# Half of the z projection inside the normalising loop, and a new order of small steps in the attention passes

## The reference, cut to what matters

```
h = rmsnorm(x, norm_pre)                       # 2048 rows of 1024
proj = h @ w_in                                # z | x,B,C | dt | q | k | v | z_sb | gates
xbc = silu(causal_conv4(xbc)); dt = softplus(dt_raw + dt_bias)
y = ssd_scan(...)                              # chunks, state carried from chunk to chunk
y = gated_group_rmsnorm(y, z, ...)             # y * silu(z), z is 2048 x 1024
o = stick_breaking(q, k, v)                    # softplus pass, sums, exponential pass, times v
out = x + rmsnorm((g1 * (y @ Wssd) + g2 * (o*silu(z_sb) @ Wsb)) @ Wout)
```

## Time and profile before

| | us |
|---|---|
| median of 3 runs | 1501.82 (1501.56 to 1502.63) |
| the profiled execution, its own time | 1497.82 |
| span of its slowest core (core 2) | 1495.9 |
| spans of the 8 cores | 1484.8 to 1495.9 |

### The profile page before, as it was taken

One profiled execution on the slowest core, in us unless ns is written; L12 is line 12 of the kernel. 1 busy time (PEld: TensorE's weight loads), 2 busy tenths in 40 slices (PEclk: granted clock), 3 DMA queues, 4 the chain that ended last, 5 costly groups with the idle time before them and its releaser, 6 DMA issues.

```text
span 1495.9 us, 22674 instructions; the slowest of 8 cores (1484.8 to 1495.9 us)
## 1 busy us (share of the span) xinstructions
PE 1286.3 (86%) x7112; PEld 539.3 (36%) x7236; DVE 833.3 (56%) x1386; ACT 858.8 (57%) x1081; POOL 106.6 (7%) x187
## 2 busy tenths in 40 slices
PE   2778987889889879889879889888777989999997
PEld 1434444323234323233323333323223434444443
DVE  2566852756756766766766666676563222322356
ACT  5446652776776776686776676777674321212122
POOL 2200000001000001000000000001001000000022
PEclk9989998999999999999999999998879999999999
DMA  9732664312121313121211012015103952153263
GB/s 238 121 72 53 106 141 103 63 35 52 53 49 42 63 34 67 39 48 56 50 34 62 29 35 62 29 35 103 44 15 72 215 108 29 15 71 29 71 225 155
DMA packets 117635, 109.34 MB, mean 73 GB/s; under 512 B 67984, under 2 KB 96016, under 8 KB 117520
## 3 DMA queue, kind: packets, MB, share of 16 engines
q1 hardware_dynamic: 65376, 83.51, 18.1%
q0 software_dynamic: 52144, 24.38, 14.2%
HBM read 103.81 MB, written 28.44 MB: 88 GB/s over the span
## 4 chain that ended last, share of the span: by engine, by line
PE 62%; ACT 18%; issue 8%; DVE 6%; DMA 5%; SPq 0%; ACTq 0%; DVEq 0%; POOL 0%; POOLq 0%
PE ps L311 15%; PE ps L1013 9%; ACT wtb L1063 9%; PE ps L1023 7%; PE ps L1029 5%; PE ps L396 5%; ACT spF L1063 4%; PE ps L1241 4%; PE ps L1210 4%; PE ps L317 4%; PE ps L1215 4%; PE ps L1080 3%; PE ps L377 3%; ACT spD L1063 2%; DMA wst<-w_in 2%
## 5 line engine op out<-in xcount | busy, mean ns | idle before, releaser
L1063 ACT ACTIVATE wtb<-ps 128x1024 bf16<-128x1024 f32 (+2 forms) x320 | 272.0, 893 | 186.4 <-PE ps L1029 172.9
L1013 PE MATMUL ps<-qT,kT 64*128 64x512 bf16 (+3 forms) x1280 | 235.5, 369 | 105.2 <-ACT wtb L1063 35.1
L311 PE MATMUL ps<-hT,wst 128*128 128x512 bf16 x1128 | 262.2, 385 | 17.8 <-DMA wst<-w_in 4.9
L1063 ACT ACTIVATE spF<-ps 128x1024 bf16<-128x1024 f32 x192 | 184.4, 1036 | 19.4 <-PE ps L1013 19.2
L1013 PEld LDWEIGHTS ps<-qT,kT 64*128 64x128 bf16 x1280 | 69.4, 93 | 280.9 <-issue 275.9
L311 PEld LDWEIGHTS ps<-hT,wst 128*128 128x128 bf16 x1152 | 113.0, 99 | 155.9 <-issue 26.9
L396 PE MATMUL ps<-hT,wst 128*128 128x512 bf16 x467 | 149.4, 396 | 12.5 <-DVE yB L842 8.7
L1029 PE MATMUL ps<-Ssum,cb 128*128 128x512 bf16 (+2 forms) x512 | 143.0, 361 | 0.0
L1224 ACT ACTIVATE gs<-ps,bgate 128x512 f32<-128x512 f32 x64 | 44.0, 688 | 172.4 <-PE ps L311 139.6
L1227 DVE TENSOR_TENSOR tt<-ps,gs 128x512 f32<-128x512 f32 x64 | 44.2, 691 | 160.2 <-ACT gs L1224 160.2
L1048 DVE TENSOR_TENSOR Ssum<-Ssum,spF 128x1024 bf16<-128x1024 bf16 x168 | 115.6, 688 | 15.1 <-DVE Ssum L1048 6.7
(11 more groups left out here) (124 smaller groups left out, 1521.6 us busy)
## 6 DMA issues: line engine op xcount, KB each, us to landing
seg<-cs_rows SPq DMA_DIRECT2D x32, 512.0 KB, 4.3
wst<-w_in POOLq DMA_DIRECT2D x32, 256.0 KB, 5.5
wst<-w_in POOLq DMA_DIRECT2D x5, 1024.0 KB, 13.2
region<-x SPq DMA_DIRECT2D x8, 512.0 KB, 13.3
xmore<-x SPq DMA_DIRECT2D x8, 512.0 KB, 13.8
sz_rows<-zst SPq DMA_DIRECT2D x16, 256.0 KB, 2.3
xs_rows<-xst SPq DMA_DIRECT2D x16, 256.0 KB, 3.2
xsc<-xs_rows SPq DMA_DIRECT2D x16, 256.0 KB, 2.9
```

What stands on the lines that cost most here:

```text
L311: K.op("pe", lambda e, c=c: e.matmul(ps[bank][:], lhsT=wt[:, c, coff:coff + 128], rhs=hT[:, c, g * 512:(g + 1) * 512], start=(c == 0), sto ...
L1013: K.op("pe", lambda e, a_=a_, pr=pr: e.matmul(ps[b0 + a_][:, q0:512], lhsT=kT[par][pr, c * 128:(c + 1) * 128], rhs=qT[par][pr, qs:qs + nq] ...
L1063: K.op("act", lambda e: e.activation(out=dst, in_=psall[:, b0:b0 + 2, q0:512], func=fn), r=[B_ps[b0], B_ps[b0 + 1]], w=[bd])
```

## The change

Four edits. (1) The z units take a row tile and a half. The 15 units of half 0 of tiles 0 to 14 are issued in the normalising loop, two in each of iterations 8 to 14 and one in 15; the other 17 stay in the convolution stage, spread more thinly. `zst` becomes four buffers of one unit each, each stored by its own DMA, and the weights of half 0 are loaded at t = 3. (2) `dt_proj` uses bank 1. (3) In phase 1 the scan step and the fill are issued ahead of `post`. (4) `sub` and `lim` of the next chunk are appended to elements 8, 9 and 10 of `ex_`, the load of its rows moves from element 7 to 2, and `sp_` is one element shorter; chunk 0 keeps them in `sp_` behind four empty elements.

```diff
-    def z_unit(u):
-        t, hf = u // 2, u % 2
-        bank = 6 + hf
+    def z_unit(t, hf):
+        k_ = zn[0] % 4
+        bank = 6 + zn[0] % 2
+        zn[0] += 1
         proj_tok(wz, [B_wz[hf]], hf * 512, 512, t, ps[bank][:], bank)
...
-            if hf == 1: K.dma("sp", sz_dr[t * 128:(t + 1) * 128, :], zs[:], r=bz, w=[B_szd[t]])
+        K.op("act", lambda e: e.activation(out=zst[k_][:], in_=ps[bank][:], func=AF.Silu), r=[B_ps[bank]], w=[B_zst[k_]])
+        K.dma("sp", sz_dr[t * 128:(t + 1) * 128, hf * 512:(hf + 1) * 512], zst[k_][:], r=[B_zst[k_]], w=[B_szd[t][hf]])
@@ dt_proj
-            proj_tok(wz, [B_wz[2]], 1024, 16, t, ps[6][:, t * 16:(t + 1) * 16], 6)
+            proj_tok(wz, [B_wz[2]], 1024, 16, t, ps[1][:, t * 16:(t + 1) * 16], 1)
@@ normalising loop
         if t >= 0:
             a_evac(t)
+        if t == 3:
+            K.dma("pool", wz[:, :, 0:512], w_in_v[:, :, 0:512], r=[B_hT[1]], w=[B_wz[0]])
         if t == 11:
...
-            for hf in range(2):
-                K.dma("pool", wz[:, :, hf * 512:(hf + 1) * 512], w_in_v[:, :, hf * 512:(hf + 1) * 512], w=[B_wz[hf]])
+            K.dma("pool", wz[:, :, 512:1024], w_in_v[:, :, 512:1024], w=[B_wz[1]])
         if t >= 4 and t % 4 < 3:
             proj_g(t % 4, t // 4 - 1, "dve")
+        if t >= 8:
+            z_unit(2 * (t - 8), 0)
+            if t < NT - 1:
+                z_unit(2 * (t - 8) + 1, 0)
@@ convolution stage
-    zq = list(range(32))
+    zq = [(15, 0)] + [(t, 1) for t in range(NT)]
         if 3 <= nb < 12:
-            z_units(1)
             proj_g(nb, 2, "act")
             proj_g(nb, 3, "act")
             z_units(1)
         if i == 0:
             dt_proj()
-            z_units(2)
+            z_units(1)
...
-            z_units(6)
+            z_units(4)
@@ scan lists
-        sp_ = [[(sub, 0)], [(sub, 1), (scores,)], [(mscf,)], [(lim, 0), (lim, 1)], [(yoff, 0), (xwf,)], [(yoffm, 0)],
-               [(yoff, 1), (yinit, 0)], [(yoffm, 1)], [(state, 0)], [(statea, 0)], [(state, 1), (yinit, 1)], [(statea, 1)],
-               [(yadd, 0)], [(yadd, 1)], [(nextload,)]]
-        ex_ = [[(expo, 0)], [(expo, 1), (attn, 0)], [(attn, 1)], [(diag, 0)], [(diaga, 0)], [(diag, 1)], [(diaga, 1), (gate, 0)],
-               [(gate, 1), (sq, 0), (nextseg,)], [(sq, 1)], [(norm, 0), (norm, 1)], [], [(tr,)], [(ev,)]]
+        pre_ = [[(sub, 0)], [(sub, 1)], [(lim, 0), (lim, 1)]]
+        sp_ = [[(scores,)], [(mscf,)], [(yoff, 0)], [(yoffm, 0)], [(yoff, 1), (xwf,)], [(yoffm, 1)], [(yinit, 0)],
+               [(state, 0)], [(statea, 0)], [(state, 1), (yinit, 1)], [(statea, 1)], [(yadd, 0)], [(yadd, 1)], [(nextload,)]]
+        ex_ = [[(expo, 0)], [(expo, 1), (attn, 0)], [(attn, 1), (nextseg,)], [(diag, 0)], [(diaga, 0)], [(diag, 1)],
+               [(diaga, 1), (gate, 0)], [(gate, 1), (sq, 0)], [(sq, 1)], [(norm, 0), (norm, 1)], [], [(tr,)], [(ev,)]]
+        if c == 0:
+            sp_ = [[], [], [], []] + pre_ + sp_
@@ attention loop
+                if lists:
+                    for m_, k_ in zip(lists[0][0], (8, 9, 10)):
+                        ex_[k_] = ex_[k_] + m_
                 queue += ex_
...
-        for T in (groups[gi - 2] if gi >= 2 else []):
-            post(T)
         if ph == 1:
             used = run_micro(queue.pop(0)) if queue else False
             ...
+        for T in (groups[gi - 2] if gi >= 2 else []):
+            post(T)
+        if ph == 1:
             for T in grp:
                 prep_qk(T)
```

More of the change, by code:

```diff
@@ L455, in build @@
     sz_dr = nc.dram_tensor("sz_rows", [L, 1024], BF16).ap()
-    B_szd = [Buf() for _ in range(NT)]
+    B_szd = [[Buf(), Buf()] for _ in range(NT)]
     xs_dr = nc.dram_tensor("xs_rows", [L, 1024], BF16).ap()
@@ L485, in build @@
     B_xcT = [Buf(), Buf()]
-    zst = [sb("zst%d" % i, [128, 1024], BF16) for i in range(2)]
-    B_zst = [[Buf(), Buf()] for _ in range(2)]
+    zst = [sb("zst%d" % i, [128, 512], BF16) for i in range(4)]
+    B_zst = [Buf() for _ in range(4)]
+    zn = [0]
     xst = [sb("xst%d" % i, [128, 8, 128], BF16) for i in range(4)]
@@ L591, in dt_proj @@
         for t in range(NT):
-            proj_tok(wz, [B_wz[2]], 1024, 16, t, ps[6][:, t * 16:(t + 1) * 16], 6)
-        K.op("dve", lambda e: e.tensor_tensor(out=dts[:, 0, :, :], in0=ps[6][:, 0:NT * 16].rearrange("p (t h) -> p t h", t=NT),
+            proj_tok(wz, [B_wz[2]], 1024, 16, t, ps[1][:, t * 16:(t + 1) * 16], 1)
+        K.op("dve", lambda e: e.tensor_tensor(out=dts[:, 0, :, :], in0=ps[1][:, 0:NT * 16].rearrange("p (t h) -> p t h", t=NT),
                                               in1=hv[:, 0:16].unsqueeze(1).to_broadcast([128, NT, 16]), op=ALU.add),
-             r=[B_ps[6], B_hv], w=[B_dts] + B_xbuf)
+             r=[B_ps[1], B_hv], w=[B_dts] + B_xbuf)
         K.op("dve", lambda e: e.tensor_scalar(out=dts[:, 2, :, :], in0=dts[:, 0, :, :], scalar1=-1.0, scalar2=None, op0=ALU.mult),
@@ L690, in z_units @@
             if zq:
-                z_unit(zq.pop(0))
+                z_unit(*zq.pop(0))
     ident(0)
@@ L793, in load_chunk @@
         K.dma("sp", btk[k_][:], bt_dr[rows, :], r=[B_btd[b][half] for b in range(2)], w=[B_btk[k_]])
-        K.dma("sp", sz[k_][:], sz_dr[rows, :], r=[B_szd[c]], w=[B_sz[k_]])
+        K.dma("sp", sz[k_][:], sz_dr[rows, :], r=B_szd[c], w=[B_sz[k_]])
     def heads(ap):
@@ L950, in nextseg @@
                 load_seg(c + 1)
-        sp_ = [[(sub, 0)], [(sub, 1), (scores,)], [(mscf,)], [(lim, 0), (lim, 1)], [(yoff, 0), (xwf,)], [(yoffm, 0)],
-               [(yoff, 1), (yinit, 0)], [(yoffm, 1)], [(state, 0)], [(statea, 0)], [(state, 1), (yinit, 1)], [(statea, 1)],
-               [(yadd, 0)], [(yadd, 1)], [(nextload,)]]
-        ex_ = [[(expo, 0)], [(expo, 1), (attn, 0)], [(attn, 1)], [(diag, 0)], [(diaga, 0)], [(diag, 1)], [(diaga, 1), (gate, 0)],
-               [(gate, 1), (sq, 0), (nextseg,)], [(sq, 1)], [(norm, 0), (norm, 1)], [], [(tr,)], [(ev,)]]
-        return sp_, ex_
+        pre_ = [[(sub, 0)], [(sub, 1)], [(lim, 0), (lim, 1)]]
[5 more added lines that the diff above has]
+            sp_ = [[], [], [], []] + pre_ + sp_
+        return pre_, sp_, ex_
     def run_micro(m):
@@ L1089, in build @@
     queue = []
-    chunk = [0]
+    lists = [ssd_lists(c) for c in range(NT)]
     for gi in range(len(groups) + 2):
@@ L1098, in build @@
             if ph == 0:
-                sp_, ex_ = ssd_lists(chunk[0])
-                chunk[0] += 1
+                pre_, sp_, ex_ = lists.pop(0)
                 queue += sp_
```

## The result

The change makes the kernel slower: 1522.54 us median (four runs) against 1502.22, as a ratio of paired runs 1.0124 [1.0102, 1.0147], or +18.6 us of 1502. The prediction was 1494.3, range 1480 to 1507: wrong in sign, and outside the range.

What follows compares the result with a forecast made beforehand. The prediction saw no single bound throughout: TensorE in the convolution stage, ACT in phase 0, a TensorE-ACT hand-over loop in phase 1. Its terms summed to -7.5 us, taking 1501.8 to 1494.3, range 1480 to 1507.

Steps and rivals of the forecast that it cites:

- Fill ahead of `post`: 0: Phase 1 of attention: `post` doesn't wait today, so issuing the fill ahead gains nothing; bounds -10 and 0 us.
- The moved steps in phase 1: +2.5: End of phase 1: DVE's idle time takes `sub(0)`, but `sub(1)` delays masks and `post` some 0.4 us; +2.5 us.
- Idle time filled: Normalising loop: moved z units fill TensorE's 7.7 us of idle time except 1.8; -5.9 us.
- new wait: Normalising loop: transposes wait behind Silu, Square and Copy on ACT, 3.1 us five times and 2.0 once; +17.5 us.
- Clock: Normalising loop: TensorE's clock falls behind five of the new waits, 1.6 us each; +8.0 us.
- Rival B: Loop: the clock stays up behind the new waits and the weights are in time; 1484 us, chance 0.20.
- Early weight load: Loop: the z weights, loading among x loads, land 20.5 us after issue, delaying the first z matmul; +2.7 us.
- Convolution stage: Convolution: dt in bank 1 and four `zst` buffers shorten TensorE's waits, the 7.84 us one to about 3.9; -5.3 us.
- First pass: First attention pass: later `scores` finds its chunk loaded, ending most of ACT's 5.34 us wait; -4.0 us.
- (2, 1) passes: Phase 0 of seven attention passes: less DVE work ends waits for a bank and at `prevbf`; 2.25 us each, -15.8.
- Rival E: Attention: DVE's relief doesn't reach ACT, as `prevbf(0)` is late for its own chain; 1507 us, chance 0.13.
- Rival C: Phase 1: the new order shortens the TensorE-ACT hand-over loop by 0.1 us in some 100 groups; 1484 us, chance 0.10.

Runs made afterwards that it cites:

- e3: The changed kernel with `post` back ahead of the scan step and the fill, all else as changed: 1503.55, ratio 1.0035 to the kernel before.
- e6: The kernel before with only `sub` and `lim` of the next chunk moved to the end of phase 1 (new lists): 1486.84, ratio 0.9877.
- e5: The kernel before with only `post` put behind the scan step and the fill: 1498.89, ratio 0.9982.
- e2: The loop and convolution stage of the kernel before with the attention stage of the changed kernel: 1493.63, ratio 0.9962.
- e4: The changed kernel with the Silu of z issued on ACT behind the next iteration's Square and Copy: median 1511.16, ratio 0.9920 to the kernel before.
- e8: The changed kernel with both the held-back Silu and `post` ahead of the fill again: 1479.11, ratio 0.9842 to the kernel before.
- e7: The changed kernel with 12 more unused matmuls of 512 columns behind the z units of iterations 8 to 14: 1514.68, ratio 1.0096 to the kernel before.
- e10: The changed kernel with dt back in bank 6: 1519.16, ratio 1.0114 to the kernel before.
- e11: e8 with the state chain issued ahead of `yinit` in phase 0, and `xwf` with `mscf`: 1452.33, ratio 0.9674 to the kernel before.
- e1: The loop and convolution stage of the changed kernel with the attention stage of the kernel before: 1520.88, ratio 1.0140.

## Why the prediction was wrong, by its own steps

Two steps of the attention half failed, and by the mean of eight cores they share its miss of 21.7 us (2.8 gained, 24.5 forecast): 12.5 of it come back when edit 3 is undone (e3), and the other 9.2 lie mainly in the (2, 1) term, sized at -15.8 where e3 has -5.0. The loop half came out some 5 us worse than its sum of +17.0, by terms that are sized below.

The first step that failed is "Fill ahead of `post`: 0", together with "The moved steps in phase 1: +2.5". I looked at what `post` waits for, its weights, and found nothing late. I didn't look at what `post` releases. It also issues the `ogst` copy on DVE, and the order change moves that copy behind `norm`, `sub(1)` and the fill's copy. The next pass needs the bank. Its bounds, -10 and 0, held no loss at all. Edit 3 undone gives 13 us back (e3); each edit without the other shows no such wait, or 0.36 of it (e6, e5). How much the collision costs depends on the core that is looked at: 20.2 of attention time between the slowest cores of after and e3, but 4.6 between those of e2 and e6, with the same waits (11.9 and 11.5). By the mean of eight cores it is 12.5 and 7.6, and 10.5 between e4 and e8; what makes these differ stays open.

The other steps, with what was measured:

- *Idle time filled, -5.9; new wait, +17.5.* Right. Five waits of 3.02 to 3.08 and one of 2.07 are 17.4; e4 takes them away and gains 24.6 with what hangs on them. The estimate of 0.5 for the Silu was 0.6.
- *Clock, +8.0.* Right: 1.3 to 1.7 behind each wait, some 7.4 on this core. e7 shows it by itself: 4.7 earlier at the start of attention, though its matmuls take 2.75 also where the wait was 2.07 or none, and its weights came 0.8 later. The rule in the Trainium skill ("TensorE: Matmul & The Clock Gate", "HAM oscillation"), by which this term would be 0, didn't hold here; the window from 60 to 70, with a wait of 3.02 in it, has a mean clock of 0.83, and on the eight cores 37 of the 40 waits of 3.02 to 3.16 were followed by a lower clock. Rival B falls.
- *Early weight load, +2.7.* 4.37: the load took 22.9 instead of 20.5. Two readings in this term were off as well: POOL issued it at 24.7, not 28, and the first z matmul was ready at 43.4, not 45.7. The turns that the DMA engines take between queues by the Trainium skill ("DMA: Bandwidth & Descriptors", "Queues, rings and completion order"), read as an even share, had given 0.
- *Convolution stage, -5.3.* Mis-sized: -1.5, the 27.8 less the 26.3 of moved work. `trans(0)` waits 4.19 (forecast 3.9), `dt_cum` 0.89 (0.7). The wait for `zst` (1.27 before) stayed, at 1.43, in spite of four buffers. And the bank of dt is worth nothing that can be measured (e10). I had credited that edit with the end of the wait of 7.84, which the removed z unit ends by itself.
- *First pass, -4.0.* Phase 0 -1.2 and its phase 1 +1.9; by the mean of eight cores -2.9 and +0.7. The clock between 300 and 310 is 0.66 on core 0 of after, behind waits of 0.82, 0.68 and 1.38; on core 2 the same three waits come 6 us earlier and the clock from 294 to 304 is 1.00. What decides between the two stays open.
- *(2, 1) passes, -15.8.* The second step that failed, and without the collision too: e3 has -5.0 in all (-4.9 by the mean of eight), 0.7 each instead of 2.25, below the lower bound of 1.1. The wait at `prevbf` that I counted as ended is there still, 2.01 at 575 in after. In after they are +10.1 (+5.2 by the mean). Rival E, which has `prevbf` late for its own chain, fits this part, and e11 shows the place: with `state(0)` issued ahead of `yinit` the phases fall to 20. e11 moves `xwf` and `yinit` too, so the chain alone wasn't tried.
- *(3, 0) passes, -7.2.* -6.4, by the mean of eight -4.7. Right in kind, and a little large.
- *Phase 1 unchanged.* 32.7 to 32.9 where it was 32.9, but for the first and the last one with a scan step (34.99 and 35.96, before 33.07 and 33.86). Rival C falls: in e5 the new order shortens most phases 1 from 32.85 to 32.74, 0.1 for a whole phase of ten groups and not for each group. The 0.1 for each group stood on no row.

The sum from the start of the attention stage on, on the slowest cores: first pass +0.7, (2, 1) +10.1, (3, 0) -6.4, the other phases 1 and the rest +0.9, so +5.3. In the seven (2, 1) phases the waits at `ogst` are 10.8 (the eighth, of 1.08, is in the last pass). That the rest of the difference to e3 (15.1) is the clock behind them is argued from the window at 448 (0.60) and not shown by itself; by the mean of eight cores the difference is 10.2, with a mean clock of 0.88 in these phases in after and 0.90 in e3. What e11 gained beyond its expectation shows in the lengths of the phases and in the clock, and wasn't taken apart.

## What to carry to other kernels

When a helper moves, look at every engine that it issues work on, the copy that it does once in many calls above all, and ask who waits for the buffer that it frees; that the helper itself never waits says nothing about it. When an in-order engine gets new work that depends on TensorE, put it behind the work that TensorE is waiting for: the same z units cost 21 us (e1) with their Silu ahead of Square and Copy, and about 30 us less with it behind (e4: 0.9920, after: 1.0124). Cost edits that touch one queue together: `sub(1)` at 1.22 turned a wait of 0.36 into one of 1.5 to 1.7.

## What was not expected of the hardware

TensorE's clock fell behind shorter waits than I had rows for: on core 0, behind 1.67 us, with 0.35 shortly ahead of it, the granted clock of the 4 us from 448 was 0.60, a mean of its levels of 1.2 and 2.4 GHz. TensorE was busy in all of these 4 us, so 4 x 0.40 = 1.6 us were lost: about as much again as the wait.

And the same wait doesn't always have this effect. Here is core 2 of the same execution, at the same place of the program, TensorE's timeline and then the window of 4 us behind:

```profile
439.68 0.36 PE L1085 MATMUL ps<-wtb,vtok 128*64 128x128 bf16 x4 [1.68 <-DVE ogst L1091]
```
```profile
440.00:444.00 4.00, 4.00 (x31) 1.59 (x30) 2.96 (x7) 2.41 (x4) 0.00 (x0) 1.00 0.19 66
```

Counted over the eight cores of after, by the granted clock of the 4 us behind each wait: of the 56 waits at `ogst` of 1.49 to 1.68, 23 were followed by a lower clock; of the eight of 1.08, none; of the 40 in the loop of 3.02 to 3.16, 37; of the eight of 2.04 to 2.08, none (in e1, three of eight). Core 0, the slowest, had the most behind `ogst`, four of seven. So a short wait can have a price on top of its length, on some cores and not on others. Which core is the slowest may hang on that; it isn't shown by itself, nor what decides whether the clock falls.

In e11, whose phase 0 from 357 on has no wait of TensorE above 0.72 on the slowest core, the clock is 1.00 in that window on all eight cores, and the TensorE work takes 17.7 us on that core (92 records) rather than the 19.8 of the pass at 558 in after (93 records).
